# Paged value cache loaded from SyncE's queue, between the projection weights, instead of from GpSimd's

## The chip, the cores and the metric

The kernel is written in Bass, with every engine's instruction stream and every semaphore wait set by hand, and runs on one core of one Trainium2 chip. TensorE (PE), VectorE (DVE), ScalarE (ACT), GpSimd (POOL) and SyncE (SP) run side by side, and 16 DMA engines move data between HBM and on-chip memory. The metric is the device time of one launch, in microseconds (us); lower is better.

## The reference, cut to what matters

Two decoder layers for a prompt of 512 tokens and for eight sample rows with one new token each, all float32, with the same weights. The part that the change touches is layer 1's stick-breaking attention of the eight sample rows over 2048 past positions each, which lie in a paged cache: 16 pages of 128 positions per sample, each page 128 x 1024 floats (512 KB) of keys and as many of values.

```python
def stick_breaking_block(q, k, v, q_pos, k_pos, offset):
    z = (jnp.einsum('bqhd,bshd->bhqs', q, k) * (q.shape[-1] ** -0.5)
         + offset.astype(jnp.float32)[None, :, None, None])
    ...
    weight = jnp.where(mask, jnp.exp(log_beta + between), 0.0)
    return jnp.einsum('bhqs,bshd->bqhd', weight, v)

# odd_layer, for the sample rows
h = rms_norm(x, norm_g) * (1.0 + scale) + shift
qc, kc, vc, gc, ud, vd, gd = split_cols(h @ w_in, ODD_SIZES)
k_past = cache_k[i][page_table].reshape(dec_b, n_past, HC, DC)
v_past = cache_v[i][page_table].reshape(dec_b, n_past, HC, DC)
```

## The kernel before, in words

Projections run on PE with activations and weights each split into a high and a low part: one tile of 128 output columns takes two "units" (halves of the 2048 inputs), and a unit is 48 matmuls of 260 columns. For each unit, SP loads 512 KB of weights into one of five slots of `raw`; ACT writes the high part (`w_hi`, line 854) and DVE the low part (`w_lo`, line 1193); each of the two has two buffers, so the split of a unit waits until PE has finished the unit two before it. SP's queue loads a slot anew once the slot's last unit is split (lines 344 to 349), and holds nothing else in this stage.

The stage around the change is called `l1b`. It has eight passes with tiles, 0 to 7, of five tiles (ten units, u0 to u9), and a pass 8 without tiles. Pass i computes the projections of head i, finishes head i - 1 of the prompt, works on the keys of sample i and on the values of sample i - 1. The passes 2 to 7 are a loop on each engine (on DVE it is line 1704). Between its units PE does a step of a second programme, `mix1`: after u0 the matmuls called p0 here (line 746; they wait for DVE's line 1611), after u1 the transposes, and after u2 to u9 the steps k = 0 to 7. Step k multiplies value pages 2k and 2k+1 with the attention weights (`m<-arena,mod`, lines 803 to 807), and counts `v_free` for each page.

DVE runs the same pattern. After PE's unit u(k+2) it copies a tile out where one is complete, splits a weight, and then takes key pages 2k and 2k+1 of the next sample (line 1553: eight multiply-and-sum instructions per page, one for each head), each of which counts `k_free`. After the last two key pages of a pass it copies the values' result out (line 1692, `orow`), which also waits for value page 15; then come the loop's branch and lines 1607 to 1611, for which PE's p0 waits.

All pages are loaded by POOL (lines 1751 to 1808) into the five slots of `pages`. Keys have slots 0 and 1: page p may be loaded when page p - 2 has been used (`k_free`). Values have slots 2, 3 and 4: page p may be loaded when page p - 3 has been used (`v_free`). POOL's stream is one order: for each k, value pages 2k+1 and 2k+2, then key pages 2k and 2k+1. Each load reads its page number from `ptab` first. In pass 8 values have all five slots. `qb` is the sample's query, copied to all partitions.

Of the kernel before, what the change touches and what calls it, by code (L numbers as in the profile page):

```python
# [16 lines left out]
NB = 8  # L17
# [7 lines left out]
NPAGE, PAGE, NPOOL = 16, 128, 160  # L25
HC = 8
# [23 lines left out]
L1B_ORDER = [TILE] * 5  # L50
# [65 lines left out]
def build(nc, a, o, cst):  # L116
    ctx = ExitStack()
    with ctx:
# [213 lines left out]
        def _(sp):  # L332
# [97 lines left out]
            weights("l1a", 0, L1A_ORDER, v["o_w_in"], l1a_cols(0))  # L430
            with sp.Fori(1, 4) as j:
                weights("l1a", j, L1A_ORDER, v["o_w_in"], l1a_cols(j), turns=(1, 4))
            weights("l1b", 0, L1B_ORDER, v["o_w_in"], l1b_cols(0))
            with sp.Fori(1, 8) as i:
                weights("l1b", i, L1B_ORDER, v["o_w_in"], l1b_cols(i), turns=(1, 8))
            weights("out1", 0, OUT_ORDER, v["o_w_out"], [0, P])
            with sp.Fori(1, 8) as j:
                weights("out1", j, OUT_ORDER, v["o_w_out"], [j * 256, j * 256 + P], turns=(1, 8))

# [23 lines left out]
        def _(pe):  # L463
# [269 lines left out]
            def mix1(i, tiles, head, values, out):  # L733
# [32 lines left out]
                for k in range(8):  # L766
                    if head and k == 0:
                        pe.wait_ge(s("tok_a"), i)
                        pe.wait_ge(s("tok_v"), i)
                        for t in range(NT):  # L770
                            mm(M[0][:, P * t:P * t + P], vntok[:, t, :], wst, start=True, stop=False)
                            last = mm(M[0][:, P * t:P * t + P], ones[0:1, :], brow[0:1, 0:P], start=False, stop=True)
                        last.then_inc(s("sg"), 1)
                    if head and k == 1:
                        pe.wait_ge(s("od"), i)
                        for b in range(NT):
                            last = mm(m012[:, SB_OFF[b]:SB_OFF[b] + T - P * b], G[0][:, P * b:P * b + P],
                                      tmp[1][:, P * b:T])
                        last.then_inc(s("z"), 1)
                    if head and k == 3:  # L780
                        pe.wait_ge(s("rest"), i)
                        for b in range(NT):
                            off = SB_OFF[b]
                            last = mm(m012[:, off:off + T - P * b], cm["from_key"][:, :], za[:, off:off + T - P * b],
                                      start=True, stop=(b == 3))
                            for l in range(b + 1, NT):
                                last = mm(m012[:, off + P * (l - b):off + T - P * b], ones[:, :],
                                          za[:, SB_OFF[l]:SB_OFF[l] + T - P * l], start=False, stop=(l == 3))
                        last.then_inc(s("between"), 1)
                    if head and k == 4:  # L790
                        pe.wait_ge(s("weight"), i)
                        for b in range(NT):
                            last = mm(M[0][:, P * b:T], vtok1[:, b, :], za[:, SB_OFF[b]:SB_OFF[b] + T - P * b],
                                      start=(b == 0), stop=(b == 3))
                        last.then_inc(s("oc"), 1)
                    if values:
                        if k == 0:
                            pe.wait_ge(s("s_weight"), i)
                            pe.wait_ge(s("tok_v"), i)
                        for p in (2 * k, 2 * k + 1):  # L800
                            slot, load = value_slot(p, tiles)
                            pe.wait_ge(s(f"page{slot}"), value_loads(i, slot, tiles) * 16 + load * 16)
                            for q in range(4):
                                last = mm(M[3][32 * q:32 * q + NB, 0:256], wv[:, 8 * p:8 * p + 8],
                                          pages[:, slot, 256 * q:256 * q + 256],
                                          start=(p == 0), stop=(p == NPAGE - 1))
                            last.then_inc(s("v_free"), 1)
                    yield
# [942 lines left out]
        def layer1_pages(pool):  # L1751
# [8 lines left out]
                pool.dma_start(pages[:, slot, :], src[bass.ds(page, 1)].rearrange("n s d -> (n s) d"))\  # L1760
                    .then_inc(s(f"page{slot}"), 16)

            def value_page(i, p, keys):
                slot, load = value_slot(p, keys)
                if not keys and slot < 2 and load == 1:
                    pool.wait_ge(s("k_free"), 128)
                elif load > 1:

                    pool.wait_ge(s("v_free"), (i - 1) * 16 + (p - (3 if keys else 5) + 1))
                    pool.sem_inc(s("pool_waited"), 1)  # L1770
                elif not (isinstance(i, int) and i == 1):
                    pool.wait_ge(s("v_free"), (i - 1) * 16 - (0, 2, 1)[p])
                    pool.sem_inc(s("pool_waited"), 1)
                fetch(cv, i - 1, p, slot)

            def body(i, keys, values):
                if values:
                    value_page(i, 0, keys)
                for k in range(8):
                    for p in (2 * k + 1, 2 * k + 2):  # L1780
                        if values and p < NPAGE:
                            value_page(i, p, keys)
                    for p in (2 * k, 2 * k + 1):
                        if keys:
                            if k:
                                pool.wait_ge(s("k_free"), i * 16 + (p - 1))
                                pool.sem_inc(s("pool_waited"), 1)
                            elif not (isinstance(i, int) and i == 0):
                                pool.wait_ge(s("k_free"), i * 16)
                                pool.sem_inc(s("pool_waited"), 1)  # L1790
                            fetch(ck, i, p, key_slot(p)[0])
                            if p == 1:
                                if isinstance(i, int) and i == 0:
                                    pool.wait_ge(s("q_out"), 16)
                                pool.dma_start(qb, q_dram[bass.ds(i, 1), :].rearrange("b n -> (b n)")
                                               .partition_broadcast(P)).then_inc(s("qb"), 16)
                    if k == 3 and keys:
                        if not (isinstance(i, int) and i == 0):
                            pool.wait_ge(s("sg"), i)
                        pool.dma_start(ws, a["o_w_s"][0, bass.ds(i, 1)].rearrange("g t s -> t (g s)"))\  # L1800
                            .then_inc(s("ws_in"), 16)
                        pool.dma_start(brow[0:1, 0:P], a["o_b_s"][0, bass.ds(i, 1)]).then_inc(s("ws_in"), 16)
# [2 lines left out]
            body(1, True, True)  # L1805
            with pool.Fori(2, NB) as i:
                body(i, True, True)
            body(NB, False, True)


        @block.gpsimd
# [128 lines left out]
```

## Time and profile before

| what | us |
|---|---|
| median of 3 runs (2479.94 to 2484.56) | 2480.41 |
| the profiled execution, its own time | 2479.76 |
| its span | 2478.2 |
| PE busy | 2238.9 (90%) |
| DVE busy | 1166.4 (47%) |
| ACT busy | 596.7 (24%) |
| POOL busy | 258.9 (10%) |
| p0 of pass 5 to p0 of pass 6 (about 1929.5 to 2023.6) | 94.1 |

The execution takes 1.6 us more than its span. "Busy" PE time counts matmuls that are running; idle time of PE in `l1b` is short and stands in the rows below. Times in the rows count from the start of the span. A DMA's landing time runs from its issue to the count on its semaphore.

### The profile page before, as it was taken

How to read it: one execution, taken by the hardware profiler on the slowest of the kernel's cores; microseconds unless marked ns; L12 is line 12 of the kernel's file. 1: busy time of each engine (PE TensorE's matmuls, PEld its weight loads, DVE VectorE, ACT ScalarE, POOL GpSimd, SP SyncE). 2: the span in 40 equal slices, each digit the busy share in tenths (PEclk: the TensorE clock that was granted, in tenths of full speed). 3: DMA queues.
4: the chain of work that ended last, by engine and by line, in shares of the span. 5: the costliest groups of instructions: out<-in, count | busy, mean ns of one | idle time of the engine just before them, and what ended most of it. 6: DMA issues, size and time to landing. Idle time of an engine off the chain costs nothing.

```text
span 2478.2 us, 46284 instructions
## 1 busy us (share of the span) xinstructions
PE 2238.9 (90%) x17191; PEld 1973.8 (80%) x17191; DVE 1166.4 (47%) x3560; ACT 596.7 (24%) x741; POOL 258.9 (10%) x429
## 2 busy tenths in 40 slices
PE   6799999999999999699979997999989889877997
PEld 2188888888888878599969997887777777755997
DVE  1543333424433342533453436767657657664332
ACT  1322121212212111222233331321321322222221
POOL 0000100101010010100000001112112112111110
PEclk9999999999999899699989998999999999988999
DMA  9977455554655555034332335778668668663442
GB/s 310 320 218 208 147 164 157 164 161 147 192 154 152 158 147 176 21 103 115 115 137 86 88 89 181 251 246 296 213 224 282 220 236 273 212 229 124 129 135 65
DMA packets 399987, 436.44 MB, mean 176 GB/s; under 512 B 16917, under 2 KB 306991, under 8 KB 399168
## 3 DMA queue, kind: packets, MB, share of 16 engines
q1 hardware_dynamic: 340838, 244.88, 33.1%
q0 software_dynamic: 49184, 180.78, 21.2%
q10 hardware_dynamic: 9810, 8.73, 1.0%
q8 instruction: 96, 1.57, 0.3%
q14 instruction: 59, 0.48, 0.1%
HBM read 407.79 MB, written 26.54 MB: 175 GB/s over the span
## 4 chain that ended last, share of the span: by engine, by line
PE 67%; DMA 11%; DVE 10%; issue 6%; ACT 3%; POOLq 2%; POOL 1%; ACTq 1%; DVEq 0%; SPq 0%
PE pt L465 52%; PE m L465 13%; DMA arena<-in_cache_k 7%; DVE arena L1553 3%; ACT arena L854 2%; DMA arena<-in_cache_v 1%; PE m L469 1%; POOLq L1759 1%; DMA raw<-in_e_w_ada 1%; ACT w_hi L854 1%; DMA arena<-in_o_k_norm_g 1%; DVE arena L1364 1%; PE pt L469 0%; DVE arena L1310 0%; DVE w_lo L1193 0%
## 5 line engine op out<-in xcount | busy, mean ns | idle before, releaser
L465 PE MATMUL pt<-act_hi,w_hi 128*128 128x260 f32 x4384 | 922.3, 292 | 54.4 <-DVE act_lo L1276 21.8
L465 PE MATMUL pt<-act_hi,w_lo 128*128 128x260 f32 x4384 | 896.1, 286 | 0.0
L465 PE MATMUL pt<-act_lo,w_hi 128*128 128x260 f32 x4384 | 896.1, 287 | 0.0
L465 PEld LDWEIGHTS pt<-act_hi,w_hi 128*128 128x128 f32 x4384 | 692.7, 194 | 118.7 <-issue 69.0
L1193 DVE TENSOR_TENSOR w_lo<-raw,w_hi 128x1024 fp32r<-128x1024 f32 x274 | 335.4, 1224 | 873.1 <-ACT w_hi L854 872.6
L465 PEld LDWEIGHTS pt<-act_lo,w_hi 128*128 128x128 f32 x4384 | 692.3, 193 | 0.0
L465 PEld LDWEIGHTS pt<-act_hi,w_lo 128*128 128x128 f32 x4384 | 690.2, 192 | 0.0
L854 ACT ACTIVATE w_hi<-raw 128x1024 fp32r<-128x1024 f32 x274 | 289.9, 1058 | 1297.7 <-PE pt L465 1283.4
L1553 DVE CUSTOM_DVE_ANT_0 arena<-arena 128x128 f32<-128x128 f32 x1024 | 225.9, 287 | 99.5 <-DMA arena<-in_cache_k 90.1
L465 PE MATMUL m<-arena 128*128 128x128 f32 (+7 forms) x1136 | 211.1, 347 | 10.5 <-POOL arena L1840 4.1
L854 ACT ACTIVATE arena<-arena 128x1040 f32<-128x1040 f32 (+8 forms) x199 | 169.1, 862 | 151.7 <-DVE arena L1670 52.3
L465 PEld LDWEIGHTS m<-arena 128*128 128x128 f32 (+3 forms) x1136 | 166.8, 213 | 46.4 <-issue 18.4
L465 PE MATMUL m<-raw,cond 128*9 128x512 f32 x768 | 132.4, 652 | 28.1 <-DMA raw<-in_e_w_ada 14.5
L465 PE MATMUL m<-arena,ones 1*128 1x128 f32 (+5 forms) x268 | 78.5, 408 | 49.8 <-DVE arena L1611 32.8
L465 PEld LDWEIGHTS m<-arena,ones 128*128 128x128 f32 (+1 forms) x268 | 50.2, 206 | 89.8 <-issue 57.0
L1840 POOL TENSOR_SCALAR arena<-arena 128x256 f32<-128x256 f32 x56 | 53.1, 949 | 487.3 <-DVE arena L1410 451.5
L1760 POOL DMA_DIRECT2D arena<-in_cache_k x128 | 67.6, 528 | 320.9 <-issue 303.7
L1760 POOL DMA_DIRECT2D arena<-in_cache_v x128 | 67.8, 530 | 312.1 <-PE m L465 230.4
L465 PE MATMUL m<-arena,mod 128*8 128x256 f32 x1024 | 72.5, 388 | 23.6 <-DMA arena<-in_cache_v 23.5
L854 ACT ACTIVATE arena<-m 128x512 f32<-128x512 f32 (+2 forms) x85 | 46.0, 571 | 166.1 <-PE m L465 139.3
L465 PEld LDWEIGHTS m<-raw,cond 128*9 128x9 f32 x768 | 16.5, 90 | 86.6 <-DMA raw<-in_e_w_ada 42.9
L1553 DVE DVE_READ_ACCUMULATOR2_ANT arena<- 128x1 f32 x1024 | 84.5, 82 | 0.0
(156 smaller groups left out, 1094.3 us busy)
## 6 DMA issues: line engine op xcount, KB each, us to landing
arena<-in_cache_k POOLq DMA_DIRECT2D x128, 512.0 KB, 4.9
arena<-in_cache_v POOLq DMA_DIRECT2D x128, 512.0 KB, 5.7
raw<-in_o_w_in SPq DMA_DIRECT2D x112, 512.0 KB, 4.3
raw<-in_e_w_in SPq DMA_DIRECT2D x98, 512.0 KB, 4.5
raw<-in_e_w_ada SPq DMA_DIRECT2D x96, 512.0 KB, 5.7
raw<-in_o_w_ada SPq DMA_DIRECT2D x96, 512.0 KB, 5.4
raw<-in_e_w_out SPq DMA_DIRECT2D x32, 512.0 KB, 3.9
raw<-in_o_w_out SPq DMA_DIRECT2D x32, 512.0 KB, 4.7
```

The source lines that it names most:

```text
L465: return pe.matmul(out, lhsT, rhs, start=start, stop=stop, skip_group_check=True)
L469: return pe.transpose(out, x, ident[0:k, 0:k])
L854: return act.activation(out, x, fn, **kw)
L1193: tt(w_lo[:, b, :], raw[:, sl, :], w_hi[:, b, :].bitcast(F32), ALU.subtract)\
L1364: return ts_(d, x, SCALE, None, ALU.mult) if to == 2 else copy(d, x)
L1553: last = dve.tensor_tensor_reduce(kpage, kpage, qb[:, P * h:P * h + P], 1.0, 0.0, ALU.mult, ALU.add, zs[:, at:at + 1])
L1759: page = pool.value_load(ptab[0:1, bass.ds(sample * NPAGE + p, 1)], min_val=0, max_val=NPOOL - 1)
L1760: pool.dma_start(pages[:, slot, :], src[bass.ds(page, 1)].rearrange("n s d -> (n s) d"))\
L1840: pool.tensor_scalar(carry[:, n, :], S[:, (n - 1) % 2, :], small[:, 6 * (n // 2) + n % 2:6 * (n // 2) + n % 2 + 1], None, ALU.mult).then_i ...
```

## The change

The value pages leave POOL's stream and go into SP's. SP issues, in each of the passes 1 to 7, one weight unit (u4 of the pass), then value pages 1, 2 and 0, then three weight units, and from there on two value pages after each weight unit. Their waits on `v_free` stay what they were, and now stand in SP's stream ahead of the next weight load. Pass 8's sixteen value pages are issued behind the first four loads of `out1`'s weights. The two slots that keys and values share in pass 8 get semaphores of their own (`value0`, `value1`). POOL keeps the key pages, `qb` and the two small loads.

```diff
-            weights("l1b", 0, L1B_ORDER, v["o_w_in"], l1b_cols(0))
-            with sp.Fori(1, 8) as i:
-                weights("l1b", i, L1B_ORDER, v["o_w_in"], l1b_cols(i), turns=(1, 8))
+            cv = a["cache_v"][0].rearrange("n s h d -> n s (h d)")
+
+            def value_page(i, p, keys):
+                slot, load_ = value_slot(p, keys)
+                if not keys and slot < 2 and load_ == 1:
+                    sp.wait_ge(s("k_free"), 128)
+                elif load_ > 1:
+                    sp.wait_ge(s("v_free"), (i - 1) * 16 + (p - (3 if keys else 5) + 1))
+                elif not (isinstance(i, int) and i == 1):
+                    sp.wait_ge(s("v_free"), (i - 1) * 16 - (0, 2, 1)[p])
+                page = sp.value_load(ptab[0:1, bass.ds((i - 1) * NPAGE + p, 1)], min_val=0, max_val=NPOOL - 1)
+                sp.dma_start(pages[:, slot, :], cv[bass.ds(page, 1)].rearrange("n s d -> (n s) d"))\
+                    .then_inc(s(f"page{slot}" if slot >= 2 else f"value{slot}"), 16)
+
+            def l1b_load(i, u):
+                load_tile("l1b", i, u, u % 2, v["o_w_in"], l1b_cols(i)[u // 2], (1, 8))
+
+            def l1b_pass(i, values=True, last=False):
+                for at_ in range(10):
+                    if at_ < 6:
+                        l1b_load(i, at_ + 4)
+                    elif not last:
+                        l1b_load(i + 1, at_ - 6)
+                    if values and at_ == 0:
+                        for p in (1, 2, 0):
+                            value_page(i, p, True)
+                    if values and at_ >= 3:
+                        for p in (2 * at_ - 3, 2 * at_ - 2):
+                            if p < NPAGE:
+                                value_page(i, p, True)
+
+            sp.wait_ge(s("ptab"), 16)
+            for u in range(4):
+                l1b_load(0, u)
+            l1b_pass(0, False)
+            l1b_pass(1)
+            with sp.Fori(2, 7) as i:
+                l1b_pass(i)
+            l1b_pass(7, True, True)
             weights("out1", 0, OUT_ORDER, v["o_w_out"], [0, P])
+            for p in range(NPAGE):
+                value_page(HC, p, False)
@@ PE, step k of mix1
-                            pe.wait_ge(s(f"page{slot}"), value_loads(i, slot, tiles) * 16 + load * 16)
+                            if slot < 2:
+                                pe.wait_ge(s(f"value{slot}"), load * 16)
+                            else:
+                                pe.wait_ge(s(f"page{slot}"), value_loads(i, slot, tiles) * 16 + load * 16)
@@ POOL, layer1_pages
             def body(i, keys, values):
-                if values:
-                    value_page(i, 0, keys)
                 for k in range(8):
-                    for p in (2 * k + 1, 2 * k + 2):
-                        if values and p < NPAGE:
-                            value_page(i, p, keys)
                     for p in (2 * k, 2 * k + 1):
...
-            body(NB, False, True)
```

POOL's stream in the loop of passes 2 to 7, a little after its middle, before (`in_cache_v` is a value page, `in_cache_k` a key page; each is a wait, the load of the page number, and the DMA):

```order
418 L1759 ISA [waits v_free]
419 L1759 TENSOR_LOAD ptab
420 L1759 ISA x2
421 L1760 ISA
422 L1760 DMA arena<-in_cache_v 128x1024
423 L1759 ISA [waits k_free]
424 L1759 TENSOR_LOAD ptab
425 L1759 ISA x2
426 L1760 ISA
427 L1760 DMA arena<-in_cache_k 128x1024
```

And POOL's stream at the like place now, where only the line numbers of the file have moved besides:

```order
261 L1800 ISA [waits k_free]
262 L1800 TENSOR_LOAD ptab
263 L1800 ISA x2
264 L1801 ISA
265 L1801 DMA arena<-in_cache_k 128x1024
266 L1800 ISA [waits k_free]
267 L1800 TENSOR_LOAD ptab
268 L1800 ISA x2
269 L1801 ISA
270 L1801 DMA arena<-in_cache_k 128x1024
```

No key page stands behind a `v_free` wait any more. SP's stream in its loop before was weight loads alone:

```order
277 L349 ISA [waits split_lo,split_hi]
278 L349 DMA raw<-in_o_w_in 128x8x128
279 L347 REGISTER_ALU
280 L349 ISA [waits split_lo,split_hi]
281 L349 DMA raw<-in_o_w_in 128x8x128
```

Now, in the second half of SP's loop (a value page needs the same five instructions as on POOL):

```order
389 L349 ISA [waits split_lo,split_hi]
390 L349 DMA raw<-in_o_w_in 128x8x128
391 L443 ISA [waits v_free]
392 L443 TENSOR_LOAD ptab
393 L443 ISA x2
394 L444 ISA
395 L444 DMA arena<-in_cache_v 128x1024
396 L443 ISA [waits v_free]
397 L443 TENSOR_LOAD ptab
398 L443 ISA x2
399 L444 ISA
400 L444 DMA arena<-in_cache_v 128x1024
```

Two waits on `v_free` now stand between a weight load and the next one.

## Rows read from the trace of the kernel before

**Rows 1.** Windows view, pass 5: busy time of each engine, clock, DMA share, GB/s
```profile
1927.70:2021.90 94.20, 85.41 (x688) 73.23 (x688) 63.86 (x320) 23.74 (x29) 18.50 (x35) 0.95 0.73 245
```

**Rows 2.** Waits view, 1642.6 to 2210 (passes 2 to 7): total us, times, longest
```profile
PE m L465 <- DVE arena L1611: 28.6, 6, 6.4
PE m L465 <- DMA arena<-in_cache_v: 16.5, 17, 2.3
PE m L465 <- DVE arena L1692: 14.0, 6, 8.2
...
DVE arena L1553 <- DMA arena<-in_cache_k: 68.7, 53, 3.1
```

**Rows 3.** Chain that ended last, pass 5's end: start, us, what
```profile
1992.07 0.94 DVE arena L1553 x9
...
2010.79 4.84 DMA arena<-in_cache_k
...
2016.55 0.90 DVE arena L1553 x9
2017.45 0.34 DVE arena L1692
2017.79 3.40 issue
...
2023.60 2.30 PE m L465 x4
```

**Rows 4.** Timeline of PE, value matmuls in pass 5: start, us, [idle before]
```profile
1966.85 0.62 PE L465 MATMUL m<-arena,mod 128*8 128x256 f32 x8 [0.65 <-DMA arena<-in_cache_v]
...
2001.60 0.62 PE L465 MATMUL m<-arena,mod 128*8 128x256 f32 x8 [0.37 <-DMA arena<-in_cache_v]
...
2008.12 0.62 PE L465 MATMUL m<-arena,mod 128*8 128x256 f32 x8
2010.39 0.62 PE L465 MATMUL m<-arena,mod 128*8 128x256 f32 x8 [1.66 <-DMA arena<-in_cache_v]
```

**Rows 5.** Timeline of POOL, last steps of pass 5: start, us, [idle before]
```profile
1994.36 0.53 POOL L1760 DMA_DIRECT2D arena<-in_cache_k  x1 [2.39 <-issue]
1995.70 0.53 POOL L1760 DMA_DIRECT2D arena<-in_cache_v  x1 [0.81 <-issue]
1997.01 0.53 POOL L1760 DMA_DIRECT2D arena<-in_cache_v  x1 [0.78 <-issue]
...
2002.27 0.53 POOL L1760 DMA_DIRECT2D arena<-in_cache_k  x1 [2.00 <-PE m L465]
2003.57 0.53 POOL L1760 DMA_DIRECT2D arena<-in_cache_v  x1 [0.78 <-issue]
2008.64 0.54 POOL L1760 DMA_DIRECT2D arena<-in_cache_k  x1 [4.54 <-issue]
```

**Rows 6.** Line 1760 in pass 0 (14 key pages); DMA view, passes 2-7: KB, us
```profile
DMA to landing us min/median/max: 3.6/4.4/5.9
...
arena<-in_cache_k POOLq DMA_DIRECT2D x96, 512.0 KB, 4.9
arena<-in_cache_v POOLq DMA_DIRECT2D x95, 512.0 KB, 5.8
```

**Rows 7.** The page's part 5: the two splits of a weight unit
```profile
L1193 DVE TENSOR_TENSOR w_lo<-raw,w_hi 128x1024 fp32r<-128x1024 f32 x274 | 335.4, 1224 | 873.1 <-ACT w_hi L854 872.6
...
L854 ACT ACTIVATE w_hi<-raw 128x1024 fp32r<-128x1024 f32 x274 | 289.9, 1058 | 1297.7 <-PE pt L465 1283.4
```

**Rows 8.** SP in pass 5 and the next start: its issues (ns), its waits (us)
```profile
L349 SPq DMA_DIRECT2D raw<-in_o_w_in x11: 372/373/378, 1930.6 to 2024.7; - x11
...
SPq L348 <- DVE w_lo L1193: 99.7, 11, 12.6
```

**Rows 9.** Pass 8: waits view of PE (2205 to 2300); timeline of POOL
```profile
PE m L465 <- DMA arena<-in_cache_v: 5.4, 3, 3.4
...
2257.35 0.53 POOL L1760 DMA_DIRECT2D arena<-in_cache_v  x1 [5.79 <-PE m L465]
```

More of the change, by code:

```diff
@@ L1761, in fetch @@
                     .then_inc(s(f"page{slot}"), 16)
[L1763 to L1774, printed above, removed]
             def body(i, keys, values):
-                if values:
-                    value_page(i, 0, keys)
                 for k in range(8):
-                    for p in (2 * k + 1, 2 * k + 2):
-                        if values and p < NPAGE:
-                            value_page(i, p, keys)
                     for p in (2 * k, 2 * k + 1):
```

## Prediction

> **What bounds the kernel now.** I read four views in this order: the waits of PE in the stage `l1b`, the chain of waits at the end of one pass, the timelines of PE and POOL beside it, and the landing times of the page loads.
>
> The change can only act in `l1b`, passes 1 to 8. In pass 5 PE is busy for 85.4 of 94.2 us [rows 1]. So the whole idle time is under 9 us a pass, and the waits view says where it is [rows 2]. Over six passes PE waits 28.6 us for DVE's line 1611 and 14.0 us for line 1692 (`orow`). Both are the same place, the matmuls p0 after u0. It waits 16.5 us for value pages.
>
> Who ends last at p0? The chain at pass 5's end [rows 3] shows it. The last key page (15) is issued at 2010.79 and lands 4.84 us later. DVE works it off until 2017.45, copies `orow`, spends 3.40 us at its loop's branch and more on lines 1607 to 1611, and PE starts p0 at 2023.60. PE's last value matmul had run at 2010.39 [rows 4] and one unit of some 6 us followed. So the end of a pass hangs on the key pages' own loop: a buffer freed, a new load issued, landed, worked off.
>
> Does POOL's queue hold that loop up? Mostly it does not. DVE frees the buffer of key page 9 at 1993.01 (1992.07 plus 0.94 [rows 3]), and POOL issues key page 11 at 1994.36 [rows 5], 1.35 us later. Two back-to-back issues on POOL stand 1.31 us apart (1995.70 and 1997.01 [rows 5]), so 1.35 us is POOL's own reaction with nothing ahead of it. Key page 15 follows in the same manner. The value pages' waits are over before the keys' turn comes. What value pages do meet on POOL is the reverse: page 15 is issued at 2003.57, behind key page 13 at 2002.27 [rows 5], though page 12, on which it waits, was used before 2001.6 [rows 4].
>
> **The change part by part.** Removed from POOL: 16 loads a pass with their waits. By the paragraph above the keys gain nothing from the shorter stream. They may gain in landing time. In pass 0, where no value page is loaded, a key page lands in 4.4 us (median of 14), in passes 2 to 7 in 4.9 (96 of them) [rows 6]. The 0.5 us is what value pages cost keys when both share POOL's DMA queue and the engines. After the change they share only the engines, so the gain per load is between 0 and 0.5; it can't be over that, since the value bytes are still moved, and it can be negative if the engines now serve the values first, by no more than the distance of keys to values today, 5.8 - 4.9 = 0.9. I take 0.5, the end nearer to a queue of its own. From unit u7 on, units follow each other faster than the keys' loop turns: key pages 11, 13 and 15 use the same buffer and are issued at 1994.36, 2002.27 and 2010.79 [rows 5, 3], 7.9 and 8.5 us apart, while the value steps 6 and 7, a unit apart, begin at 2000.6 (page 13's 2001.60 less a wait of 0.37 and page 12's 0.62) and at 2008.12 [rows 4], 7.5 apart. So three landings in a row count fully at the end of a pass: 3 x 0.5 = 1.5 us.
>
> This is capped. DVE takes key pages 14 and 15 only after it has split the weight that u9 makes room for. u9 ends at 2008.1 [rows 4]; ACT's split is 1.06 and DVE's 1.22 [rows 7], so DVE can start at 2010.4 at best. Two pages are 2 x 1.8 = 3.6 us (0.94 us for nine of a page's sixteen instructions [rows 3], so some 1.8 for a page), then 0.34 for `orow`, and from there to p0 it is 2023.60 - 2017.79 = 5.8 [rows 3]. That gives 2010.4 + 3.6 + 0.3 + 5.8 = 2020.1, against 2023.60: at most 3.5 us a pass.
>
> Added to SP: the same 16 loads. SP's part of a weight load is 0.37 us, and SP stands waiting 99.7 us for splits in the stretch of eleven loads, a whole pass and its next start [rows 8]; there is room. A value page needs the load of its number too. By POOL's 1.31 for the pair, less 0.53 for POOL's DMA instruction and plus 0.37, I put SP's reaction at 1.1 us, with 0.5 and 2.5 as bounds (half of, and twice, POOL's).
>
> Queued behind a waiting value page on SP is the next weight load. The load of unit u(n+4) now goes out after the value pages freed by the step behind u(n-1). It is split only when u(n+2) is done, three units of 6 us and more later, and lands in some 6 us, as value pages do. Cost nothing, and if a value wait were longer by 10 us still nothing.
>
> The value pages themselves: the odd pages are the tight ones. Page 2k+3 may be loaded when 2k is used and is wanted one unit later, about 7 us (6 of the unit, 1 of the value matmuls). Today page 15 is issued 2.3 us after its slot is free (2003.57 against 2001.2, by rows 5 and 4), a page with a free queue no sooner than after 1.3, and it lands in 5.8 [rows 6]. So it misses by a little: 0.65, 0.37 and 1.66 us in pass 5 [rows 4]. With 1.1 + 5.8 = 6.9 it just makes it. The wait of 1.66 lies in the shadow of DVE's longer way to p0 and brings nothing; ten of the 16.5 us are of that kind if the other five passes are like this one. The rest, 6.5 / 6 = 1.1 us a pass, is on the path. But the 0.37 of it falls after u7, where the keys' loop ends last again. I count 0.7.
>
> Pass 8 has no keys. PE waits 5.4 us for value pages there, the last three of them issued from 2257.35 on, 1.2 us apart [rows 9]. At SP's pace (1.1) and with a quicker reaction I count 1.0 us, bounds 0 and 3.
>
> Sum: seven passes x (1.5 + 0.7) = 15.4, and 1.0: 16.4 us. The profiled execution took 2479.76, 0.65 under the median of the runs; 2479.76 - 16.4 = 2463.4. I say 2463.
>
> A rule of the Trainium skill speaks against the first term: "DMA: Bandwidth & Descriptors", section "Issuing engines are not separate DMA queues", says that transfers started by different engines run on the same 16 engines and interleave, and that spreading them saves only the issue time. By that rule landings stay as they are, the 1.5 is gone, and the sum is the first rival's. The same page's section "Queues, rings and completion order" says that each DMA engine takes turns between the queues that have work, a packet at a time. By that a key page alone in its queue would no longer stand behind two value pages, and the difference between passes 0 and 2 to 7 agrees in sign, though there the value bytes are absent altogether.
>
> **The rivals.** (a) No shorter landings: keys keep 4.9 us. Then only the value waits go, 7 x 0.7 + 1.0 = 5.9 at most, and since a pass's end hangs on the keys' loop some of it is taken back: 2474 to 2480. For it: a DMA share of 0.73 of the engines at 245 GB/s [rows 1], which the change leaves alone. Against it: pass 0.
>
> (b) Everything that can go goes: the tail's cap of 3.5, all 1.1 of value waits, 3 in pass 8: 7 x 4.6 + 3 = 35, 2445. It needs key landings near 3.8 us even beside value loads. For it: the quickest key pages of pass 0 land in 3.6 [rows 6]. Against it: key page 15 took 4.84 [rows 3], although POOL had issued no value page after 2003.57, only key page 14 at 2008.64 [rows 5].
>
> (c) Slower: value pages lose their turn. On SP they come in bursts of two with a weight load behind, while keys in the other queue take half of the engines. If a value landing grows by the 1.3 us by which a second key page lands later than a single one (4.84 [rows 3] against 3.6 [rows 6]), the odd pages come 1.1 + 7.1 = 8.2 after their slot is free, and PE waits 1.2 us in a step. Keys are in flight for about three of the five steps from k = 2 to 6: 3.6 a pass against 1.1 today, 7 x 2.5 = 17.5, so 2497. It decides from a median landing of values of 6.2 us, or from a reaction of SP of 1.5. For it: values already take 0.9 longer than keys. Against it: no key is ahead of them in their queue any more.
>
> (d) The value pages' move does nothing for PE since value and key bytes collide as before and both effects cancel: this is (a) with 0, counted there.
>
> **How the numbers follow.** Forecast case 0.57, with a range of its own of 2454 to 2473; (b) 0.14; (a) 0.16; (c) 0.13. A difference of 0.2%, 5 us, is what a measurement of this kernel can tell from none. (a) lies mostly within it (its end of 2474 is just outside), (c) mostly above: faster 0.73, same 0.15, slower 0.12. The range that leaves out two in ten: the low end at (b)'s 2445, the high end at 2482, where half of the "same" case and all of the "slower" one are left out.
>
> **What the profile of the changed kernel would show.** The keys' median landing in passes 2 to 7 at 4.4 (at 4.9 the first term is wrong). PE's waits for value pages from 16.5 down to a few us in the same six passes; if they rise, (c). PE's waits for lines 1611 and 1692, together 42.6 today, lower by some 9. SP issuing each value page about 1.1 us after its slot is free. Weight splits waiting for no load. The distance of two p0 at 92, from 94.1. The prediction is wrong if the distance stays, or if a wait for `raw` appears on ACT.

## The result, and the profile after

The changed kernel takes 2520.8 us (median of 4 runs, 2518.24 to 2532.15). The kernel before took 2480.18 (4 runs) beside it. The ratio is 1.0173, with an interval of 1.0137 to 1.0208: slower, by 40 us, where 17 us of gain were forecast. The profiled executions have spans of 2516.7 and 2478.2 us; of the 38.5 between them, 27.8 lie in passes 2 to 7, 7.1 in pass 1, 3.0 ahead of it and 0.6 behind pass 7. So the loss is one of the steady passes.

The windows view below is of the changed kernel, with the columns of [rows 1]: pass 5 alone, and passes 2 to 7 together.

```profile
1951.51:2050.84 99.33, 88.45 (x688) 76.87 (x689) 63.48 (x320) 23.74 (x29) 10.12 (x19) 0.91 0.71 230
1652.90:2248.80 595.90, 517.46 (x4080) 449.34 (x4080) 381.37 (x1915) 141.53 (x174) 60.31 (x114) 0.91 0.70 231
```

The same six passes of the kernel before:

```profile
1642.80:2210.90 568.10, 508.37 (x4080) 435.61 (x4080) 382.43 (x1915) 141.29 (x173) 110.97 (x211) 0.95 0.74 245
```

The distance of two p0 went from 94.2 [rows 1] to 99.3. The work is the same to the instruction (4080 matmuls, 1915 of DVE). PE is busy 9.1 us longer at a clock of 0.91 instead of 0.95, and idle for 78.4 us instead of 59.7 (window less busy time). The two make up the 27.8.

The waits view of the changed kernel in those passes (total us, times, longest) says where PE's idle time is. Line 1652 is 1611 of [rows 2], line 1733 is `orow` (1692), 1738 is DVE's copy of the transposed tile, and 1594 is DVE's work on a key page (1553).

```profile
PE m L503 <- DVE arena L1652: 27.1, 6, 6.8
PE m L503 <- DVE arena L1733: 26.4, 6, 16.1
PE pt L503 <- DVE arena L1738: 23.7, 6, 6.3
PE m L503 <- DMA arena<-in_cache_v: 1.1, 3, 0.7
...
DVE arena L1594 <- DMA arena<-in_cache_k: 89.0, 44, 5.1
```

Against [rows 2] there are three movements. The wait for value pages, 16.5 us, is gone but for 1.1. `orow` grew from 14.0 to 26.4. And there is a wait that the kernel before has once in these passes, with 0.6 us: a weight unit that can't start because DVE is late with its copy, 23.7. All that grew is DVE's, and DVE itself waits 89.0 us for key pages, before 68.7. The value pages come in time now; the keys don't.

The DMA view (KB of a load, median us from issue to landing) seems to deny this:

```profile
arena<-in_cache_v SPq DMA_DIRECT2D x97, 512.0 KB, 5.5
arena<-in_cache_k POOLq DMA_DIRECT2D x96, 512.0 KB, 4.8
raw<-in_o_w_in SPq DMA_DIRECT2D x53, 512.0 KB, 6.9
```

The keys' median is 4.8, and 4.9 before [rows 6]. The weight loads went from 5.6 to 6.9. The chain that ended last, at the end of pass 5 (start, us, what), shows what the median hides:

```profile
1991.06 6.56 DMA arena<-in_cache_k
...
2009.03 6.78 DMA arena<-in_cache_k
...
2018.97 6.94 DMA arena<-in_cache_k
...
2029.08 4.88 DMA arena<-in_cache_k
...
2037.12 7.42 DMA arena<-in_cache_k
...
2045.45 0.90 DVE arena L1594 x9
...
2050.84 1.21 PE m L503
```

Five key pages stand in this chain with 4.88 to 7.42 us each. In the same part of pass 5 before, the chain holds key pages of 4.93, 5.37 and 4.84 us (the last in [rows 3]). Over passes 2 to 7 the chain runs through 25 key pages before, with a median of 5.1, and through 24 now, with a median of 6.8. (A chain picks late loads by its nature; over all 96 key pages the mean went only from 5.0 to 5.1.)

Which loads these are comes out when the pages of a step are told apart. The second of the two is issued 1.3 to 6.9 us behind the first. Mean landing in the eight steps of passes 2 to 7, read load by load, 48 pages of each kind: first pages 4.7 before (8 above 6 us) and 4.5 now (5); second pages 5.3 before (8 above 6 us) and 5.7 now (21). Nearly half of the second pages are late, and the median over all pages falls between the two heaps.

A case of it: the second key page at 2009.03 (6.78 us in the chain). SP's timeline at that moment (start, us, what it issued):

```profile
2009.76 1.50 SPq L444 DMA_DIRECT2D arena<-in_cache_v  x2
2011.58 0.38 SPq L349 DMA_DIRECT2D raw<-in_o_w_in  x1
```

Two value pages and a weight tile are issued within 2.6 us behind the key page, 1.5 MB in the other queue. Before, the value pages were issued behind it in the key's own queue, as at 2003.57 behind 2002.27 in [rows 5]; that key page took 5.37 us.

The same count over all key pages of passes 2 to 7, from the issues and landings in the trace: 58 of the 96 have three or more 512 KB loads of the other queue still in flight at their issue, or issued within 3 us behind it. They land in 5.7 us (mean), and all 26 pages above 6 us are among them. The other 38 land in 4.2. In the kernel before no key page has three such loads beside it, and 16 take more than 6 us, with other pages ahead of them in their own queue.

What a late key page does to PE is in its timeline (start, us, instruction, [idle before it]) and, for the clock, in the windows view of the same microseconds, both of the changed kernel:

```profile
2016.04 0.62 PE L503 MATMUL m<-arena,mod 128*8 128x256 f32 x8 [0.22 <-DMA arena<-in_cache_v]
2019.19 0.77 PE L503 MATMUL pt<-act_hi,w_hi 128*128 128x260 f32 x2 [2.53 <-DVE arena L1738]
...
2024.53 0.63 PE L503 MATMUL pt<-act_hi,w_hi 128*128 128x260 f32 x2
2024.97 0.44 PE L503 MATMUL pt<-act_lo,w_hi 128*128 128x260 f32 x2
```

```profile
2009.30:2015.20 5.90, 5.90 (x52) 5.77 (x49) 1.79 (x16) 0.00 (x0) 0.79 (x2) 1.00 0.78 267
2019.20:2023.20 4.00, 4.00 (x18) 4.00 (x19) 3.28 (x18) 0.00 (x0) 0.30 (x1) 0.50 1.01 371
2023.20:2027.20 4.00, 4.00 (x29) 4.00 (x28) 1.26 (x11) 0.00 (x0) 0.53 (x1) 0.77 0.84 280
```

PE waits 2.53 us for the copy, and the unit behind it starts at a granted clock of 0.50 (1.2 GHz): a pair of matmuls takes 0.64 us and not 0.40 until 2024.97. The unit takes 8.5 us, the one before the wait 5.9. One idle of 2.5 us costs 5.1. There are five such waits, of 2.5 to 6.3 us, in passes 2 to 7, with units of 8.5 to 8.6 us (four times) and 7.6 us behind them, some 12 us more than five undisturbed ones. That covers the 9.1 us of longer busy time. Before, PE's longest wait inside pass 5 was the 1.66 us of [rows 4], and the clock behind it had not fallen; the windows view of the kernel before, there and behind the long wait at p0:

```profile
2012.05:2016.05 4.00, 4.00 (x35) 4.00 (x35) 2.17 (x19) 0.00 (x0) 1.58 (x3) 1.00 0.92 277
...
2023.60:2027.60 4.00, 4.00 (x13) 2.88 (x14) 1.39 (x3) 0.98 (x3) 0.00 (x0) 0.50 0.87 309
```

The fall at p0 is in both kernels. The one inside a pass is rare before: a single such wait, 2.26 us for a value page at 1812.81, has a clock of 0.70 and a unit of 7.5 us behind it.

### The profile page after: what moved, and what is told of

It reads as the page before. It is cut to its first block, busy times and chain, and to the rows that moved or that the text cites. A ratio compares the mean times of both kernels' runs of the same rounds, so it can differ in the third digit from the quotient of the medians.

```text
span 2516.7 us, 46074 instructions
## 1 busy us (share of the span) xinstructions
PE 2253.8 (90%) x17191; PEld 1994.5 (79%) x17191; DVE 1164.4 (46%) x3560; ACT 596.5 (24%) x741; POOL 191.5 (8%) x301
## 4 chain that ended last, share of the span: by engine, by line
PE 66%; DVE 12%; DMA 11%; issue 5%; ACT 3%; POOLq 1%; ACTq 0%; SPq 0%; POOL 0%; DVEq 0%
PE pt L503 51%; PE m L503 12%; DMA arena<-in_cache_k 8%; DVE arena L1594 4%; ACT arena L895 1%; PE m L507 1%; ACT w_hi L895 1%; DMA raw<-in_e_w_ada 1%; POOLq L1800 1%; DMA arena<-in_o_k_norm_g 1%; DVE w_lo L1234 1%; DVE arena L1405 1%; PE pt L507 0%; DVE arena L1351 0%; DVE arena L1458 0%
## 5 line engine op out<-in xcount | busy, mean ns | idle before, releaser
L503 PEld LDWEIGHTS pt<-act_lo,w_hi 128*128 128x128 f32 x4384 | 699.4, 195 | 0.0
L1594 DVE CUSTOM_DVE_ANT_0 arena<-arena 128x128 f32<-128x128 f32 x1024 | 225.4, 286 | 131.8 <-DMA arena<-in_cache_k 122.0
L507 PE MATMUL m<-c_ident,arena 128*128 128x128 f32 (+3 forms) x347 | 52.1, 293 | 32.6 <-DVE arena L1433 12.1
```

The costliest lines, as they stand in the source:

```text
L503: return pe.matmul(out, lhsT, rhs, start=start, stop=stop, skip_group_check=True)
L507: return pe.transpose(out, x, ident[0:k, 0:k])
L1594: last = dve.tensor_tensor_reduce(kpage, kpage, qb[:, P * h:P * h + P], 1.0, 0.0, ALU.mult, ALU.add, zs[:, at:at + 1])
```

## The experiments

Two theories stood at first. A: the bytes of the value pages, now in another queue than the keys, make key pages land later. B: SP's order does it. Weight loads stand behind value waits, and those of the stage after pass 7 behind pass 7's last value pages; ACT waits 17.7 us for them in the changed kernel. The ratios are to the kernel before, run beside each; "passes" are distances of two p0.

**The late weights alone (e1).** The changed kernel, with the next stage's first four weight loads between the value pages of pass 7:

```diff
                     elif not last:
                         l1b_load(i + 1, at_ - 6)
+                    else:
+                        load_tile("out1", 0, at_ - 6, at_ % 2, v["o_w_out"], (0, P)[(at_ - 6) // 2])
...
             l1b_pass(7, True, True)
-            weights("out1", 0, OUT_ORDER, v["o_w_out"], [0, P])
```

> The changed kernel, with the first four loads of out1's weights placed between pass 7's value pages, where earlier passes have the next pass's loads, instead of behind value page 15. Theory A (key pages land later because value pages now come at the same time in another queue): the passes 2 to 7 stay about 99 us long; only pass 7's end gains, PE's wait for line orow there falling from 16 to 8 us: 2513. Theory B (weight loads held up behind value pages' waits in SP's queue cost the whole loss): 2480 to 2490.

2528.82 us, ratio 1.0197 (1.0148 to 1.0246). ACT's wait for these weights is gone and no time came back: the distance over the end of pass 7 stayed 97.8, and PE still waits 11.2 us for `orow` there (16.1 in the changed kernel). The 8 us that were hoped for are a miss, and the part of B that has a row in the profile costs nothing here.

**Value pages of an eighth (e2, e3).** Both leave out part of the computation's data: only 128 of a value page's 1024 columns are loaded, 64 KB for 512. e2 does it to the changed kernel (below), e3 the same to the kernel before.

```diff
-                sp.dma_start(pages[:, slot, :], cv[bass.ds(page, 1)].rearrange("n s d -> (n s) d"))\
+                sp.dma_start(pages[:, slot, 0:P], cv[bass.ds(page, 1)].rearrange("n s d -> (n s) d")[:, 0:P])\
```

> The changed kernel, where a value page's load brings only the first 128 of its 1024 columns (64 KB), so the attention output is made from other data; issues, waits and their order stay. Theory A (bytes of the values share the engines with the keys): keys land in 4.4 us median or less, the pass is 92 us or shorter, the time 2475 or less although out1's loads are still late (7 us). Theory B (order and waits in SP's queue): still 2510 to 2521.

> The kernel before, where a value page's load brings only the first 128 of its 1024 columns (64 KB); the base for the run with small values on SP. Theory A: some 5 to 7 us under that run at most (out1's late loads), so 2462 to 2470, with key landings of the same median in both. Theory B: 30 us or more under it, as the full pages are.

e2: 2470.57 us, 0.9959 (0.9924 to 0.9994). e3: 2459.31, 0.9905 (0.9888 to 0.9921). SP's instructions and waits are all there in e2, and most of the loss isn't: 11 us are left between the two kernels where there were 40. The waits view of e2, six passes:

```profile
PE m L503 <- DVE arena L1652: 21.8, 6, 5.2
PE m L503 <- DVE arena L1733: 18.2, 6, 12.9
PE pt L503 <- DVE arena L1738: 8.7, 7, 2.9
...
DVE arena L1594 <- DMA arena<-in_cache_k: 63.2, 50, 3.4
```

DVE's wait for keys is 63.2 for 89.0, the new wait 8.7 for 23.7. So it is the bytes: A, for some seven tenths by the ratios (0.54% is left between e2 and e3 where there was 1.73%; the intervals allow half to nine tenths). Of the 14.2 us by which the profiled passes 2 to 7 of e2 are longer than e3's, 6.0 lie over the end of pass 7, where e2's ACT still waits 13.6 us for the late weights of the next stage. B's part, free in e1, may cost something once the keys are quick.

**Half of the value pages (e4).** Odd value pages on SP, even ones, page 0 and pass 8 on POOL as before (its core; the rest is the bookkeeping of semaphores):

```diff
                     if values and at_ >= 3:
-                        for p in (2 * at_ - 3, 2 * at_ - 2):
-                            if p < NPAGE:
-                                value_page(i, p, True)
+                        value_page(i, 2 * at_ - 3, True)
```

> Only the odd value pages (one unit of slack) are issued by SyncE; even ones, page 0 and pass 8's stay on GpSimd ahead of the keys as before. Theory A: half of the value bytes share with the keys, so half of the loss of the passes, 2495 to 2500, with PE's waits for value pages still near 1 us in six passes, or less loss if the page beside a key matters more than the pair. Theory B: SP's order of waits is nearly the changed kernel's, so 2515 to 2521.

2512.9 us, 1.0116 (1.0081 to 1.0151). DVE waits 93.0 us for keys and PE 27.8 for its copy. Half of the change brings some two thirds of the loss; it was expected nearer to the middle. The weight tile is in the other queue before, too; one value page beside it is enough for most of the harm.

**Value pages held back (e5, e8).** If the collision is the cause, moving the value pages in time should remove it. e5 makes SP wait until the second key page of the step has landed; e8 reads the page's number once more, so that the first value page comes about 0.6 and the second about 1.2 us later.

```diff
                     if values and at_ >= 3:
+                        sp.wait_ge(s("page1"), i * 128 + 16 * (at_ - 2))
                         for p in (2 * at_ - 3, 2 * at_ - 2):
```

> The changed kernel, where SyncE, from step 0 on, issues the two value pages freed by a step only once the odd key page of the same step has landed, so keys no longer meet values that were issued after them. Theory A (keys in flight share the engines with values that come a moment later in another queue): the keys' waits on DVE fall from 89 to 70 us or less in six passes and their landings over 6 us vanish; PE's waits for value pages come up instead, to 15 us or more; 2480 to 2505. Theory C (SyncE's stream as such is slow, whatever the bytes do): 2521 or more, key waits unchanged.

```diff
+                sp.value_load(ptab[0:1, bass.ds((i - 1) * NPAGE + p, 1)], min_val=0, max_val=NPOOL - 1)
                 page = sp.value_load(ptab[0:1, bass.ds((i - 1) * NPAGE + p, 1)], min_val=0, max_val=NPOOL - 1)
```

> The changed kernel with one more read of the page number ahead of each value page on SyncE, so that a value page is issued about 0.6 us later after its slot is free, the second of a pair 1.2 us later, and the weight load behind them too: GpSimd's pace before. If it is the values' haste that hurts, key waits on DVE fall from 89 to 70 to 75 us in six passes, 2485 to 2500. If what hurts is that values and keys are in two queues, it stays at 2515 to 2525.

e5: 2584.99 us, 1.0391 (1.0346 to 1.0435), far from what A expected. The waits view, six passes:

```profile
PE m L504 <- DMA arena<-in_cache_v: 65.9, 28, 5.1
PE m L504 <- DVE arena L1653: 23.8, 6, 5.3
PE m L504 <- DVE arena L1734: 15.6, 1, 15.6
...
DVE arena L1595 <- DMA arena<-in_cache_k: 115.5, 39, 5.9
```

PE now waits for values, and the keys wait longer too, with a median landing of 5.9 (47 of 96 above 6 us, where A expected none): held back, the value pages fall on the next keys. e8: 2521.55 us, 1.0157 (1.0099 to 1.0214), no change; DVE waits 99.6 us for keys. In pass 5 the key page at 2006.88 takes 7.06 us with the value pages issued at 2007.66 and 1.7 us later. With the DMA engines busy for 0.70 of the time, there may be no quiet moment to move them to; these two runs found none. What is left of A to be tested is the queue.

**One queue for all (e6).** Keys, values and weights on SP, in the order weight, two values, two keys; the weights of the next stage as in e1. POOL keeps the query copy (`qb`, 512 KB) and two small loads.

```diff
+            def key_page(i, p):
+                if p >= 2:
+                    sp.wait_ge(s("k_free"), i * 16 + (p - 1))
+                elif not (isinstance(i, int) and i == 0):
+                    sp.wait_ge(s("k_free"), i * 16)
+                page = sp.value_load(ptab[0:1, bass.ds(i * NPAGE + p, 1)], min_val=0, max_val=NPOOL - 1)
+                sp.dma_start(pages[:, key_slot(p)[0], :], ck[bass.ds(page, 1)].rearrange("n s d -> (n s) d"))\
+                    .then_inc(s(f"page{key_slot(p)[0]}"), 16)
...
                             if p < NPAGE:
                                 value_page(i, p, True)
+                    if at_ >= 2 and not (isinstance(i, int) and i == 0 and at_ == 2):
+                        for p in (2 * at_ - 4, 2 * at_ - 3):
+                            key_page(i, p)
```

> The changed kernel with the key pages moved to SyncE too, behind the value pages of the step as GpSimd had them before, and out1's first loads between pass 7's pages; GpSimd keeps the query copy and two small loads. Keys, values and weights are then in one queue, in one order. Theory A, in the form that separate queues do the harm: key waits on DVE back at 70 us or less, 2465 to 2485. If it is only that values are issued sooner and their bytes stand ahead of the keys: key waits stay near 90 us, 2510 to 2525.

2464.32 us (2455.81 to 2467.81), 0.9895 (0.9847 to 0.9943): faster than both kernels. Its windows view of passes 2 to 7, its waits there, and its chain at the end of pass 5:

```profile
1643.10:2189.00 545.90, 504.19 (x4080) 434.31 (x4080) 382.96 (x1915) 141.06 (x174) 8.97 (x17) 0.97 0.76 254
```

```profile
DVE arena L1613 <- DMA arena<-in_cache_k: 30.7, 41, 1.6
...
PE m L522 <- DVE arena L1671: 30.2, 6, 6.0
PE m L522 <- DMA arena<-in_cache_v: 6.6, 9, 1.5
PE m L522 <- DVE arena L1752: 4.8, 1, 4.8
```

```profile
1973.53 4.34 DMA arena<-in_cache_k
...
1980.51 5.66 DMA arena<-in_cache_k
...
1988.79 5.25 DMA arena<-in_cache_k
...
1996.67 4.59 DMA arena<-in_cache_k
```

PE waits little for value pages (6.6 us), and no key page of the chain is late. In steps 1 to 7 one of 42 second pages takes over 6 us (6.02; mean 4.8), where 21 of 42 did. DVE waits 30.7 us for keys, `orow` holds PE once, the copy never, and the clock is 0.97. So neither the early value pages nor SP's longer stream does the harm by itself.

The first step of a pass is the exception. All landings of the key pages in these passes (min/median/max), and SP's issues at the start of step 0 in pass 5:

```profile
DMA to landing us min/median/max: 3.3/4.7/10.1
```

```profile
1906.68 2.75 SPq L444 DMA_DIRECT2D arena<-in_cache_v  x3
1909.79 1.48 SPq L349 DMA_DIRECT2D raw<-in_o_w_in  x2
1912.20 4.31 SPq L455 DMA_DIRECT2D arena<-in_cache_k  x2
```

Behind three value pages and two weight tiles of its own queue, with the query copy in POOL's, key page 0 lands in 8.9 to 10.1 us in all six passes, and the DMA instruction alone holds SP for 2.7 to 4.3 us, where the median key page's takes 0.33. Key page 1 behind it lands in 5.1 to 7.6. One queue doesn't shield a load from what is ahead of it; the chain doesn't pass there.

**Swapped (e7).** Keys on SP (with the function of e6), value pages on POOL: still two queues, but the weights now share the keys'.

```diff
-                    if values and at_ >= 3:
-                        for p in (2 * at_ - 3, 2 * at_ - 2):
-                            if p < NPAGE:
-                                value_page(i, p, True)
+                    if at_ >= 2 and not (isinstance(i, int) and i == 0 and at_ == 2):
+                        for p in (2 * at_ - 4, 2 * at_ - 3):
+                            key_page(i, p)
```

> Key pages on SyncE between the weights, value pages alone on GpSimd (the change the other way round; out1's first loads between pass 7's pages). Theory A, separate queues: keys and values still share, so it is slower than the kernel before, 2490 to 2510. If the values' early issue is what hurts, GpSimd's slower pace for values and SyncE's quicker one for keys (0.9 against 1.35 us from a free buffer to the issue) help: 2465 to 2480.

2468.55 us (7 runs, 2462.35 to 2495.99), 0.993 (0.9896 to 0.9964). A expected it slower than the kernel before, and it is faster: "values in another queue than the keys" is not by itself what costs the time. Its profile is of its slowest execution (2495.99), so I read only the direction: DVE waits 63.5 us for keys and PE 9.7 for values. Three things differ from the changed kernel: weight tiles no longer come from the other queue, the keys are in SP's queue, which is of another kind than POOL's (see "What stays open"), and SP reacts faster than POOL. A freed key buffer is reloaded after 0.8 us on SP (median of 84 in e6), after 1.35 on POOL ([rows 3, 5], as the prediction worked out).

**How much is reaction, how much order (e9, e10).** Both are e6 with one edit. e9 reads the page number twice ahead of each key page; e10 puts the second value page of a step behind the keys.

```diff
                     sp.wait_ge(s("k_free"), i * 16)
+                sp.value_load(ptab[0:1, bass.ds(i * NPAGE + p, 1)], min_val=0, max_val=NPOOL - 1)
                 page = sp.value_load(ptab[0:1, bass.ds(i * NPAGE + p, 1)], min_val=0, max_val=NPOOL - 1)
```

> All pages on SyncE, with one more read of the page number ahead of each key page, which takes back SyncE's quicker reaction to a free key buffer (0.9 to about 1.5 us). If the gain of that kernel over the one before is the quicker reaction, the passes lengthen from 91 to 94 us and the time is 2475 to 2485. If it is the common queue, it stays at 2464 to 2470.

```diff
-                        for p in (2 * at_ - 3, 2 * at_ - 2):
-                            if p < NPAGE:
-                                value_page(i, p, True)
+                        value_page(i, 2 * at_ - 3, True)
...
+                    if values and 3 <= at_ < 9:
+                        value_page(i, 2 * at_ - 2, True)
```

> All pages on SyncE, with the second value page of a step, which has a unit more of slack, issued behind the key pages instead of ahead of them. If bytes ahead of the keys in the one queue still cost, key waits on DVE fall from 31 to 20 to 25 us in six passes and the time is 2455 to 2463; if keys there are limited by their own loop, no change, 2464.

e9: 2473.13 us, 0.9935 (0.9906 to 0.9963); DVE's wait for keys is 56.0 for 30.7. A freed key buffer is now reloaded after 1.4 us (median of 84), which is POOL's pace, and two fifths of e6's gain are gone by the ratios (0.4% of 1.05%), though the intervals overlap. Not all of that is the keys' reaction: PE's waits for value pages rose from 6.6 to 15.6 us, since the value pages stand in the same stream. Nor is what is left all the common queue's: SP's quickest key pages take 3.3 us from issue to landing, POOL's 3.6. As an estimate, 0.3 us for each of the four key pages that the chain has in a pass (25 in six) makes some 8 us over seven passes, half of e9's 16.

e10: 2484.5 us, 0.9988 (0.9966 to 1.0011), where 2455 to 2463 had been expected. Its waits view, six passes:

```profile
PE m L522 <- DMA arena<-in_cache_v: 25.6, 20, 3.1
PE m L522 <- DVE arena L1671: 24.6, 5, 6.0
DVE arena L1613 <- DMA arena<-in_cache_k: 18.0, 24, 2.5
PE m L522 <- DVE arena L1752: 5.2, 1, 5.2
```

The keys did gain, more than expected: DVE's wait for them fell from 30.7 to 18.0, so a value page ahead of the keys in the one queue does cost them. But the value page, now behind two waits for key buffers, comes late: 25.6 us for 6.6. In one queue the order of the stream is the schedule, and it can be wrong too.

## Why the prediction was wrong

**Views and bound: right.** The end of a pass hangs on the loop of the two key buffers, and key landings are on it. That is why the change cost so much.

**Keys' landings: wrong, and this is the step that failed.** The prediction took the gain as 0.5 us a landing, with a worsening of at most 0.9, and put the gain at 1.5 us a pass. The landings in the chain went from 5.1 to 6.8 (medians), beyond the bound of 0.9. The error was to read the half microsecond between pass 0 and the later passes as the price of sharing POOL's queue. e3 shows what it was. There keys and values share the queue as before, only the value bytes are cut to an eighth, and the keys of passes 2 to 7 land in pass 0's 4.4 (KB, median us):

```profile
arena<-in_cache_k POOLq DMA_DIRECT2D x95, 512.0 KB, 4.4
```

So it is the price of bytes in flight, and the queue kept that price low, since a value page issued behind a key page cost it little. The row for this was there: keys and values are of one size, and in [rows 6] keys land in 4.9 and values in 5.8. Moved to the other queue, the value pages run beside the key page together with the weight. A key page with little beside it lands in 3.7 (the least of the changed kernel is 3.6), and most late ones of the chain in 6.6 to 7.4, some twice that; that each queue then gets half is a guess. e6 shows the reverse: second key pages at 4.2 to 4.6 in many steps, with a weight and two value pages issued behind them in their own queue.

**The sign in which the median was trusted.** The prediction said that its first term would be wrong if the keys' median stayed at 4.9. It stayed (4.8), which told that the gain was absent, but not that the chain's loads grew by 1.7. The median was a weak sign to watch, because it is mostly the second page of a step, half of the loads, that was hit, and of those nearly half.

**Value waits: right in kind.** PE's waits for value pages went from 16.5 us to 1.1. The prediction counted 0.7 us a pass as gain; 2.6 a pass of wait went, and all of it came back as waits for DVE. In pass 8, where there are no keys, the wait went from 5.4 to 5.1, not by the 1.0 taken.

**SP's reaction and room: right.** SP issues about 1.0 us after a slot is free (1.1 taken), and two value pages stand 1.17 us apart (1.31 on POOL). **Weight loads "cost nothing": right in sum.** They land in 6.9 for 5.6, and none holds a split in the passes; the weights behind pass 7 do come late (17.7 us of ACT's waits), which the prediction had not seen, and e1 shows that this costs nothing while the pages are full.

**What it said the profile would show.** Lines 1611 and 1692 lower by 9 from 42.6: they are 53.5, and line 1738 adds 23.7. A distance of 92: it is 99.3. **The clock** was in no term. A new wait of 2.5 us or more is paid twice, once as idle and once at the lower granted clock; 9.1 of the 27.8 us in passes 2 to 7 are that.

**The rivals.** (c), slower to 2497, had the collision but took the value pages for its victim. They land sooner than before (5.5 for 5.8), and the keys are hit. Neither of its signs came: values in 6.2 us, or a reaction of 1.5 (it is 1.0). Its 1.3 us is 1.24 by its own rows, which changes nothing. (a) fails with the keys' landings in the chain, (b) with them all the more.

The sentence of the Trainium skill that the prediction weighed ("DMA: Bandwidth & Descriptors", section "Issuing engines are not separate DMA queues": spreading transfers saves only issue time) holds in that no bandwidth was won: the same bytes went at 231 GB/s, before at 245. It doesn't hold as "only": where a load stands moved the key landings on the chain by 1.7 us and the kernel by 1.7%, and the measurement decides. The same page's "Queues, rings and completion order" has the engines take turns among queues, which agrees in direction with e6 against the changed kernel.

**What stays open.** That the value bytes in flight beside the keys make them late is shown (e2 against e3, and the count by load). That it is the separate queue as such is not. e6 changes the queue, the keys' reaction and what is ahead of them at once; e4 loses more than half with half of the pages; e7, with all value pages in another queue than the keys, beats the kernel before. No run had keys alone in SP's queue, or weights alone in a third one.

A rival stands that no run separates: the two queues are of different kinds. In part 3 of the page POOL's loads are in a queue named software_dynamic and SP's in one named hardware_dynamic; the 67.1 MB of value pages went from the first to the second (packets, MB, share), before and then now:

```profile
q0 software_dynamic: 49184, 180.78, 21.2%
```

```profile
q0 software_dynamic: 30752, 113.67, 13.2%
```

In all runs with a loss the keys were in the software queue and the value pages that hurt them in the hardware queue; with the kinds exchanged (e7) there was none. It may be that the software queue loses where both are full, and not that two queues are worse than one. Keys and value pages in two queues of one kind would tell.

The 11 us left between e2 and e3 are explained in part at most, by the weights behind pass 7. Nor is e6's gain split between queue, reaction and SP's quicker landings better than by e9.

## What to carry to other kernels

Ask of every load that is moved to another engine's queue which load it used to stand behind. In these runs a load on the critical loop lost little to what was issued behind it in its own queue, and much to three or more loads beside it in another (e7 warns that this isn't so for every pair of queues). What is ahead of it in its own queue costs it too. Here the urgent and the patient loads did best in one queue, in order of need. And read landing times where the chain passes, by the place of the load in its step: a median over all loads of a kind can stay put while those on the chain grow by a third.

## What the runs showed of the hardware that was not expected

- A 512 KB page lands in 3.6 to 3.8 us when little else is in flight, and in 6.6 to 7.4 when 1.5 to 2.0 MB are issued in the other queue between 2.3 us before it and 2.6 us behind it (pages of the chain in pass 5 of the changed kernel; keys in POOL's queue, the rest in SP's). With 1.0 MB or less beside them, 38 key pages landed in 4.2 (mean), none above 6.
- One queue for all pages and weights was enough: in e6 it moved 131.8 of 138.9 MB in passes 2 to 7, 254 GB/s in all, with key pages, value pages and weights landing in 4.7, 5.6 and 6.1 us (medians). With five loads issued ahead of it within 6 us, a page took up to 10.1 us and its DMA instruction held SP for up to 4.3.
- A wait of 2.53 us on PE was followed by some 5.8 us at a granted clock of 0.50, so that a unit of 5.9 us took 8.5; a wait of 2.26 us was followed by 4 us at 0.70, one of 1.66 us by 4 us at 1.00.
- A load whose address is read from a table goes out 0.8 us after its buffer is free on SP, 1.35 on POOL; two in a row stand 1.17 and 1.31 us apart. One more read of the table word makes the 1.17 on SP 1.73 (e8). From issue to landing SP's quickest key pages take 3.3 us, POOL's 3.6.
